# The second half of a gated FFN as a seven-product block multiplication over all token tiles

## The reference, cut to what matters

```
h = norm(x) * (1 + scale2) + shift2
g, u = split(h @ w_gu)              # 2 x 2816 columns
f = silu(conv3(g)) * u              # (tokens, 2816)
x = layer_norm(alpha * x + gate2 * (f @ w_down)) * ln2_g + ln2_b
```

## Time and profile before

| | |
|---|---|
| three timed runs | 2961.13, 2961.4, 2963.22 us; median 2961.4 |
| profiled execution, its own time | 2957.74 us |
| its span, first to last instruction | 2955.9 us |
| granted TensorE clock, mean over the span | 0.963 of full speed |
| PE busy | 2725.3 us (92%) |
| DVE, ACT, POOL busy | 1769.5, 1232.2, 471.0 us |

### The profile page before, as it was taken

How to read it: one execution, slowest core, us unless ns; L and a number is a source line. 1 busy time by engine, 2 the same in 40 slices (tenths; PEclk the granted TensorE clock), 3 DMA queues, 4 the chain that set the end, 5 groups by cost and what they waited for, 6 DMA issues and landing times. The chain is left out here.

```text
span 2955.9 us, 50052 instructions
## 1 busy us (share of the span) xinstructions
PE 2725.3 (92%) x17011; PEld 2475.6 (84%) x17011; DVE 1769.5 (60%) x3030; ACT 1232.2 (42%) x2612; POOL 471.0 (16%) x678
## 2 busy tenths in 40 slices
PE   4999999676999978996999999999999979999996
PEld 4999999565888866885999999999999968888875
DVE  4534332346999974777887876667666534352445
ACT  2211111115988971234555565556555522112121
POOL 0000000124444431223001000000000000230312
PEclk8999999887999998997999999999999989999999
DMA  8223222498675814563655564444444354334233
GB/s 290 82 92 120 79 92 64 169 358 176 137 153 118 162 50 149 185 197 86 226 176 170 166 205 151 151 153 149 151 151 155 107 173 139 107 128 139 85 126 130
DMA packets 400709, 435.71 MB, mean 147 GB/s; under 512 B 122592, under 2 KB 293654, under 8 KB 397848
## 3 DMA queue, kind: packets, MB, share of 16 engines
q1 hardware_dynamic: 377216, 414.28, 46.7%
q10 hardware_dynamic: 21016, 11.29, 1.3%
q0 software_dynamic: 2304, 7.88, 0.8%
HBM read 311.18 MB, written 124.57 MB: 147 GB/s over the span
## 5 line engine op out<-in xcount | busy, mean ns | idle before, releaser
L2202 PE MATMUL fu_alpha<-fu_h,fu_w 128*128 128x384 f32 x3168 | 576.3, 336 | 17.8 <-DVE fu_h L2428 10.6
L2688 PE MATMUL fd_acc<-fd_w,fd_f 128*128 128x512 f32 x2376 | 546.7, 392 | 28.5 <-DVE fd_w L2716 19.1
L2202 PEld LDWEIGHTS fu_alpha<-fu_h,fu_w 128*128 128x128 f32 x3168 | 555.1, 189 | 20.4 <-issue 20.3
L2688 PEld LDWEIGHTS fd_acc<-fd_w,fd_f 128*128 128x128 f32 x2376 | 447.4, 189 | 127.8 <-issue 19.1
L2202 PE MATMUL fu_beta<-fu_h,fu_w 128*128 128x384 f32 x1584 | 287.1, 335 | 0.6 <-DVE fu_h L2428 0.6
L2202 PEld LDWEIGHTS fu_beta<-fu_h,fu_w 128*128 128x128 f32 x1584 | 277.1, 189 | 1.1 <-issue 1.1
L598 PE MATMUL pj_gps<-pj_ht,w_in 128*128 128x256 f32 x2160 | 268.9, 285 | 0.0
L598 PEld LDWEIGHTS pj_gps<-pj_ht,w_in 128*128 128x128 f32 x2160 | 263.5, 191 | 1.3
L2712 DVE TENSOR_TENSOR fd_f<-fd_f_stage,fd_f 128x512 fp32r<-128x512 f32 (+1 forms) x110 | 91.5, 833 | 284.7 <-ACT fd_f L2668 284.7
L2668 ACT CAST fd_f<-fd_f_stage 128x512 fp32r<-128x512 f32 (+1 forms) x110 | 63.5, 579 | 443.5 <-PE fd_acc L2688 395.5
L2402 DVE TENSOR_TENSOR fu_w<-up_w_stage,fu_w 128x512 fp32r<-128x512 f32 x264 | 181.7, 689 | 85.6 <-ACT fu_w L2266 83.6
(11 more groups left out here) (221 smaller groups left out, 4125.6 us busy)
## 6 DMA issues: line engine op xcount, KB each, us to landing
up_w_stage<-in_w_gu_dram SPq DMA_DIRECT2D x88, 512.0 KB, 4.1
fu_w_sums<-w_gu_sums SPq DMA_DIRECT2D x132, 256.0 KB, 3.9
fd_w_stage<-in_w_down_dram SPq DMA_DIRECT2D x54, 512.0 KB, 3.7
fd_f_stage<-f_t SPq DMA_DIRECT2D x88, 256.0 KB, 2.6
at_k<-k_t SPq DMA_DIRECT2D x28, 704.0 KB, 13.0
w_gu_sums<-fu_w_sums SPq DMA_DIRECT2D x66, 256.0 KB, 4.8
fo_w<-in_w_ada_dram SPq DMA_DIRECT2D x8, 2048.0 KB, 18.1
up_w_stage<-in_w_gu_dram SPq DMA_DIRECT2D x44, 256.0 KB, 4.3
```

The costliest lines, as they stand in the source:

```text
L2202: mm = pe.matmul(out, w[x][:, j, k, :], b[y][:, j, k, :], start=opens and (k, x, y) == (0, HI, HI), stop=(k, x, y) == (KH - 1, LO, HI), sk ...
L2688: mm = pe.matmul(acc[:, t, at], f[a][:, slot, t * P:(t + 1) * P], w[b][:, w_at(st, slot), at], start=is_step(st, 0) and (a, b) == (HI, HI) ...
```

## The change

`f_t` becomes an array by token tile: (18 tiles, 128 channels-in-slice, 22 slices, 128 tokens). The first half's `store` writes it with two DMAs for a step of the first span and three for the others: whole tiles (runs of 128 tokens), the last tile without its last token, and the one token that belongs to the tile ahead (128 elements of 4 bytes).

The second half is rewritten. The rows of f are taken in 9 pairs of tiles (context is the ninth pair), its 2816 channels in two halves of 11 slices, and `w_down`'s 1024 columns in two halves of 512. For each pair the 2 x 2 by 2 x 2 block product is made from seven products of half size instead of eight. The loop is outermost over the seven products (`ORDER` 5, 3, 1, 4, 7, 2, 6) and inside it over the nine pairs, which makes 63 units. A unit is one 128-token operand, the sum or difference of two blocks of f for five of the seven products, times 11 slices of weights, which are a sum or difference of two blocks of `w_down` for five of the seven: 11 x 3 = 33 matmuls of 128 x 128 by 512, 2079 in all, in one PSUM bank; eight banks are used in turn.

Residual rows for all 18 tiles stay in SBUF (`res`), loaded in the first nine units and scaled by alpha on ACT. After a unit DVE multiplies its PSUM sum by the gate into `tmp` and adds or subtracts that in the places of `res` where the product belongs. A tile is complete after product 7 (the first of each pair) or 6 (the second), and then its statistics and its normalisation (now on ACT) and the two POOL operations follow. SP loads two units ahead, into three slots, with the second block of a sum in a single buffer `f_more`. POOL makes the sums of weights.

The diff, cut to what is spoken of:

```diff
@@ ffn_up_phase, store
-                    rows = bass.ds(f * P, P)
-                    t0 = p * SPAN - 1
-                    if p == 0:
-                        sp.dma_start(f_t[rows, 0:SPAN - 1], res[:, par, 1:SPAN]).then_inc(stored[par], 16)
...
+                    if p:
+                            sp.dma_start(f_t[t0 - 1, :, bass.ds(f, 1), last:P].rearrange("p f c -> p (f c)"), res[:, par, 0:1]).then_inc(stored[par], 16)
+                    if p < SPANS - 1:
+                        sp.dma_start(tiles(per_span - 1), of_tiles(c0, per_span - 1)).then_inc(stored[par], 16)
+                        sp.dma_start(f_t[t0 + per_span - 1, :, bass.ds(f, 1), 0:last].rearrange("p f c -> p (f c)"),
+                                     res[:, par, c0 + (per_span - 1) * P:SPAN]).then_inc(stored[par], 16)
...
@@ ffn_down_phase: sizes
+    SUMS = {5: ((0, 0, ALU.subtract), (0, 1, ALU.add)), 3: ((0, 1, ALU.add), (1, 1, ALU.add)), 1: ((0, 0, ALU.add), (1, 1, ALU.add)),
+            4: ((0, 0, ALU.add), (1, 0, ALU.add)), 7: ((0, 0, ALU.add),), 2: ((1, 0, ALU.add), (1, 1, ALU.subtract)), 6: ((1, 1, ALU.add),)}
+    EARLY = {3: ((0, 1),), 7: ((0, 0),), 6: ((1, 0), (1, 1))}
+    AHEAD = 6
+    RING = KH + AHEAD
+    WSLOTS, XSLOTS, HSLOTS, BANKS = 3, 3, 2, 8
...
@@ SP
+                def load_unit(u):
+                    if u >= XSLOTS:
+                        sp.wait_ge(unit_done, u - XSLOTS + 1)
+                    load_f(u)
+                    if sums_f(u) and u:
+                        sp.wait_ge(f_summed, sum_count(u) - 1)
+                        load_more(u, more_staged)
+                for u in range(UNITS):
+                    if u + 2 < UNITS:
+                        load_unit(u + 2)
+                    for b in slices_first(u + 1) + slices(u + 1):
+                        load_w(b)
+                    if u + 1 < PAIRS:
+                        load_x(u + 1)
+                    if has_tail(u - 4):
+                        store(u - 4)
...
@@ ACT
+                def normalise(u):
+                    act.wait_ge(shift_done, n + 1)
+                    act.activation(res[:, t, :], res[:, t, :], ACT.Identity, bias=shift[:, n % 4:n % 4 + 1],
+                                   scale=rstd[:, n % 4:n % 4 + 1]).then_inc(normed, 1)
...
@@ DVE
+                def sum_f(u, piece=0):
+                    dve.tensor_tensor(f_raw[:, s, k0:k1, :], f_raw[:, s, k0:k1, :], f_more[:, k0:k1, :], A_OF[form(u)][2]).then_inc(f_summed, 1)
+                def low_f(u, piece=0):
+                    dve.tensor_tensor(f_lo[:, u % XSLOTS, k0:k1, :], f_raw[:, u % XSLOTS, k0:k1, :],
+                                      f_hi[:, u % HSLOTS, k0:k1, :].bitcast(F32), ALU.subtract).then_inc(f_low, 1)
+                def gate_product(u):
+                        last = dve.tensor_tensor(tmp[:, n, :], acc[:, u % BANKS, :], gate[:, c, half(nh)], ALU.mult)
+                def add_product(u):
+                        dve.tensor_tensor(at, at, tmp[:, columns.index(nh), :], op).then_inc(added, 1)
+                for u in range(UNITS):
+                    for b in slices_first(u):
+                        low_w(b)
+                    if u:
+                        gate_product(u - 1)
+                    if u + 1 < UNITS:
+                        low_f(u + 1)
+                    if u:
+                        add_product(u - 1)
+                        statistics(u - 1)
+                    for b in slices(u):
+                        low_w(b)
+                    if u + 2 < UNITS:
+                        sum_f(u + 2)
+                    if has_tail(u - 1):
+                        negative_offset(u - 1)
...
@@ POOL
+                def affine(u):
+                    pool.wait_ge(normed, n + 1)
+                    pool.tensor_tensor(res[:, t, :], res[:, t, :], ln_g[:, :], ALU.mult).then_inc(scaled, 1)
+                    pool.wait_ge(scaled, n + 1)
+                    pool.tensor_tensor(res[:, t, :], res[:, t, :], ln_b[:, :], ALU.add).then_inc(out_done, 1)
+                for u in range(UNITS):
+                    for b in slices_first(u) + slices(u):
+                        sum_w(b)
+                    if has_tail(u - 1):
+                        make_rstd(u - 1)
+                    if has_tail(u - 2):
+                        affine(u - 2)
...
```

More of the change, by code:

```diff
@@ L2585, in ffn_down_phase @@
-        out_tiles = out_all.rearrange("(t p) d -> t p d", p=P)
[L2587 to L2617, removed]
[L2619 to L2626 removed]
+        acc = ps("fd_acc", [P, BANKS, NH])
@@ new lines, in ffn_down_phase, with pieces, f_count, sum_count @@
+        vec = lambda t: LAT if t < T_LAT // P else CTX
+        sums_f = lambda u: A_OF[form(u)][1] is not None
+        sums_w = lambda b: B_OF[ORDER[b // KH]][1] is not None
+        def pieces(u):
+            return PIECES if u == 0 else ((0, KH),)
+        def f_count(u, piece=0):
+            return piece + 1 if u == 0 else len(PIECES) + u
+        def sum_count(u, piece=0):
+            return piece + 1 if u == 0 else len(PIECES) + sum(sums_f(n) for n in range(1, u + 1))
+        def f_loads(u):
+            return sum(n > 0 for n in range(u % XSLOTS, u + 1, XSLOTS))
@@ new lines, in w_loads @@
+        def w_loads(b):
+            return sum(2 if sums_w(n) else 1 for n in range(KH + (b - KH) % WSLOTS, b + 1, WSLOTS))
+        w_sum_count = lambda b: sum(sums_w(n) for n in range(b + 1))
+        add_count = lambda u: sum(len(SUMS[form(n)]) for n in range(u + 1))
+        stats_count = lambda u: sum(len(EARLY.get(form(n), ())) for n in range(u + 1))
+        has_tail = lambda u: u >= 0 and form(u) in TAILS
+        tail_count = lambda u: sum(has_tail(n) for n in range(u))
+        tile_of = lambda u: 2 * pair(u) + TAILS.index(form(u))
@@ new lines, in slices_first, with slices, w_source @@
+        def slices_first(u):
+            j, i = divmod(u, PAIRS)
+            return [j * KH + k for k in (KH - 2, KH - 1)] if i == 0 and 0 < j < len(ORDER) else []
+        def slices(u):
+            j, i = divmod(u, PAIRS)
+            if j >= len(ORDER) - 1:
+                return []
+            if i == PAIRS - 1:
+                return [(j + 1) * KH + k for k in range(AHEAD, KH - 2)]
+            return [(j + 1) * KH + i - 2] if 2 <= i < 2 + AHEAD else []
+        def w_source(b):
+            if b < KH:
+                return res[:, STAGED_AT + b // 2, (b % 2) * NH:(b % 2 + 1) * NH]
+            return wst[:, (b - KH) % WSLOTS, 0, :]
@@ L2653, in store, with load_f @@
[L2653 to L2659 removed]
+                def load_f(u):
+                    (r, kh), _, _ = A_OF[form(u)]
+                    t = 2 * pair(u) + r
+                    for n, (k0, k1) in enumerate(pieces(u)):
+                        sp.dma_start(f_raw[:, u % XSLOTS, k0:k1, :], f_blocks[kh, t][:, k0:k1, :]).then_inc(f_staged[u % XSLOTS] if u else f_first[n], 16)
+                        if u == 0:
+                            load_more(u, f_first[n], k0, k1)
@@ new lines, in load_w @@
+                def load_w(b):
+                    s = (b - KH) % WSLOTS
+                    if b - KH >= WSLOTS:
+                        sp.wait_ge(w_low, b - WSLOTS + 1)
+                    first, second, _ = B_OF[ORDER[b // KH]]
+                    for at, block_of in enumerate((first, second)):
+                        if block_of is not None:
+                            kh, nh = block_of
+                            sp.dma_start(wst[:, s, at, :], w_blocks[kh, b % KH][:, half(nh)]).then_inc(w_staged[s], 16)
```

391 lines of the change are left out of this document (229 added, 162 removed).

## The result

The changed kernel takes 2968.6 us (median of 8 runs, 2964.0 to 2974.7) where the kernel before takes 2960.95 (8 runs): a ratio of 1.0032, 95% interval 1.0019 to 1.0045. It is slower by 0.32%, more than the 0.2% that I count as no change, though the lower end of the interval, 0.19%, still lies inside that; I had predicted 2932, a gain. The profiled execution of after has a span of 2966.6 us, 10.7 more than that of before.

A forecast was written before the change was run, and what follows sets the result against it. It took PE to bound the phase: -67.1 - 22.7 + 19 + 37 + 3 + 2 - 2 + 1 = -29.8, a span of 2926 for 2955.9, or 2932 us taken from the median; its own range was 2915 to 2950, chance 0.5.

The forecast's parts named there:

- PE: Second half of the FFN: 2079 matmuls in place of 2376 take 469.2 us, 7.45 a unit, a gain of 67.1.
- Units of products 5, 1 and 2: Units with two blocks of f: DVE needs 6.6 us of PE's 7.45 and keeps up; products 1 and 2 run at PE's pace.
- the loop: Rival, chance 0.15: single buffer f_more makes load and sum alternate, binding from a 5.2 us landing; slower from 6.8, 2993 near 8.
- The first nine units, +19: Product 5 at the second half's start: bound by DMA, 86 us after the first matmul where PE's pace gives 67.0.
- the rival of short runs: Chance 0.15: loads of f go as 512-byte pieces at 257 GB/s, first nine units lose 15 us more; total 2952.
- Products 7 and 6, +37: Tile tails: DVE and POOL operations take turns, rounds of 11.0 us, 3.55 over PE's; 24 us from product 7, 13 from 6.
- the cold last unit, +2: Product 6's last unit: only there does PE pay for a lower clock after the tail rounds' gaps, 2 us.
- slip into gaps: Rival, chance 0.2: in the tails POOL's two operations mostly meet gate products, statistics and waits; the 37 us fall away, total 2895.
- The floor of 9.3 us a round: Product 7's tails: by an exclusive lock alone, a round is no shorter than its locked operations; the 37 would be about 19.
- Changes of product, +3: Six changes between products: DVE waits for the last two weight slices, loaded only when staging slots free; half a microsecond each.
- The end, -2: After the last matmul: one tile instead of two, with POOL's two operations between DVE's last two; 14 us for 16.1.
- The first half's store, +1: First half: more store DMAs per step, their issue hidden by 4.1 us of SP idle time; only the last store shows, 1 us.

The follow-up runs named there:

- e1: Changed kernel with each tail's one-column negative offset moved from DVE to ACT as two small operations; ratio 1.0018 to the kernel before.
- e3: Changed kernel with all seven products using the first one's weights, no slice loaded, summed or split after the first unit; ratio 0.9893 to the kernel before.
- e4: Changed kernel without POOL's gain and bias operations on 17 of 18 tiles, one column copied instead; ratio 0.9875 to the kernel before.
- e5: Changed kernel with every tile's gain and bias on DVE instead of POOL, without negative offset and ACT's normalisation; ratio 0.9929 to the kernel before.
- e2: Changed kernel with weight low parts ahead of the additions on DVE and weight high parts ahead of residual scaling on ACT; ratio 1.0001 to the kernel before.

## Why the prediction was wrong

Three readings ahead of the terms were off. The pace of 225.7 ns took all 443 matmuls of the window for starts; 441 start in it, one each 226.7. The 2467 for the end of the ninth unit is 2469 by its own figures (2411.5, six times 8.4, and 7.45). The 257 GB/s came from a stretch whose bytes are nearly all in packets of 2048 bytes (595 of its 967), so it is no price for pieces of 512.

Term by term, in the profiled execution:

- *PE*: 471.2 us for 469.2; right but for the pace, which is the same in both kernels.
- *Units of products 5, 1 and 2*: right. Units 3 to 9 of product 1 took 7.48 each, with sums of 1.62. The second block of f lands 5.4 us after its issue on the median, over the 5.2 from which I had the loop bind and under the 6.8 from which it decides. One sign of that rival was there: in five of the seven units DVE's sum waited for the second block, 5.6 us in all. PE had the slack for it and lost nothing, so the rival did not come.
- *The first nine units, +19*: 13.6. Not DMA's rate all along but units 0 and 1 (17.0 and 11.0 us; of the 13.0 over two units' pace 5.5 are waits, nearly all of the rest is the lower clock); the third unit began 28.0 us after the first matmul for my 30.5, and from there PE kept its pace with DMA full, where I had 8.4 us a unit. The backlog was paid at the change to product 3 instead, through the residual on ACT. 378 GB/s there, and no packet between 512 bytes and 2 KB among the 8922 of that stretch, rule out the rival of short runs.
- *Products 7 and 6, +37, and the cold last unit, +2*: 36.1 (31.0, and 5.1 of the 8.0 at product 2, 2.9 being left there without the tails). The rounds were 10.4 to 10.7 us for 11.0. POOL did not slip into gaps. The turns were right, the operations that have to wait were not: I had the low part and the addition held, by 1.6 and 2.35, and in after it is the negative offset and the low part, by 2.2 and 1.8. I had left the offset out for its size; that the sums agree is in part luck, since whatever DVE has next of that kind is held (e1). The exclusive lock that the Trainium skill states (SBUF — State Buffer, Who interferes with whom) agrees with these rows. The floor of 9.3 us a round that I worked out beside it was not reached; the order of waiting made the longer one.
- ***Changes of product, +3*: 35.6.** This is the step that failed. I saw that the last two slices wait for staging places and gave half a microsecond to each change. I never laid the chain out. At product 4: place free 5.3 us into the last unit, two blocks a slice landing, POOL, ACT, DVE, 10.0 us; PE wants slice 10 some 14.3 us into that unit (7.48 and ten elevenths of the next), and it came at 15.4. At the other changes the places come free later, 7.1 to 12.5 us into the unit, and the last low part ends after 15.6 to 21.4. Of the 35.6, 11.1 stand at product 3, where the first nine units' backlog adds to it. Nor did I look at what stands behind the waiting instruction, the low part of the next f, nor charge the clock after each wait. That new weights make these waits is shown by e3, where the changes to 3, 1, 4, 7 and 6 are at 0. The trace of before showed the lower clock after a gap; I applied it to the last unit alone.
- *The end, -2*: +5.6 (21.7 for 16.1). DVE reached the last matmul's result at 2950.2, 5.4 us late, since the rounds were bound by DVE and POOL and not by PE, and POOL's two operations on the tile before then ran behind DVE's. e4 and e5 bring the end to 9.4 and 12.7.
- *The first half's store, +1*: the last store shows as forecast: from its first DMA to the second half's first instruction 3.2 us before and 4.0 after. Otherwise nothing can be told. From its first matmul to its last the half takes 977.8 us before, 979.7 after (1.9 more, 0.9 over the forecast) and 976.2 to 980.0 in the experiments.
- Not in the sum: 4.2 us in the phases ahead of the first half, where the code is the same in both, and 1.4 from the half's last matmul to the next one's first, the last store's 0.8 among them.

The errors: +2.0 - 5.4 - 2.9 + 32.6 + 7.6 + 0.9 + 4.2 + 1.4 = +40.4, and 2926 + 40.4 = 2966.4 for a span of 2966.6. Without the one failed step the same sum gives 2934, 22 us under the span of before. The chance of 0.14 that I gave to slower stood on another mechanism.

## What to carry to other kernels

A product with fewer matmuls moves work into what is changed between the stages: write each change out as a chain (place free, issue, landing, every engine in its order, and what is queued behind) against the moment at which PE wants it, and add the clock to the waits, here some 0.5 us for each microsecond, on the mean. Where two engines wait for each other in turn, moving a small operation only moves the wait; giving the whole job to the faster one, 2.6 us on DVE for 4.8 on POOL, brought 30 us. Leaving each suspect out once, and then both, tells whether their costs add up.

## What was not expected of the hardware

- A DVE operation over one column takes as long as the POOL operation that it meets: 2.34 us at 2930.65, and 0.16 at 2880.25 in the same kernel, where POOL was idle. Its size is no bound on its price.
- What a wait of one to two microseconds costs at the clock is not steady. Before the second unit of product 4 a wait of 1.85 us was followed by a granted clock of 0.82 (after), one of 1.58 by 1.00 (e2); before that of product 1 the same 1.33 us was followed by 1.00 in after and by 0.83 in e1. In the tails of after, waits of 2.7 and 1.1 us alternate, with 0.82 and 1.00. So a chain shortened by 1.6 us could give 3.2 back.
